# Expert rows moved by index tables, and rope halves exchanged by on-chip DMA, in a two-layer mixer and MoE trunk

## The reference

```python
h = layer_norm(x)
for l in range(2):
    m = hybrid_mixer(h, ...)           # three attentions d, s, f, gated, w_o
    h = layer_norm(ALPHA * h + m)
    f = grouped_moe(h, ...)
    h = layer_norm(ALPHA * h + f)
```

## Time and profile before

| what | value |
|---|---|
| runs | 2792.02 us median of 3 (2791.88 to 2793.4) |
| profiled execution | 2794.2 us, its span 2792.3 us |
| PE busy | 2209.5 us (79%) |
| DVE, ACT, POOL busy | 920.5, 532.5, 206.2 us |
| DMA moved | 569.59 MB, mean 204 GB/s |
| mean granted PE clock | 0.906 of full speed |

### The profile page before, as it was taken

How to read it: one execution, slowest core, us unless ns; L and a number is a source line. 1 busy time by engine, 2 the same in 40 slices (tenths; PEclk the granted TensorE clock), 3 DMA queues, 4 the chain that set the end, 5 groups by cost and what they waited for, 6 DMA issues and landing times.

```text
span 2792.3 us, 29623 instructions
## 1 busy us (share of the span) xinstructions
PE 2209.5 (79%) x9808; PEld 1253.0 (45%) x9816; DVE 920.5 (33%) x1844; ACT 532.5 (19%) x1132; POOL 206.2 (7%) x354
## 2 busy tenths in 40 slices
PE   4889979989938777777478899799898477777772
PEld 3656746756413222222156567467564122222221
DVE  5656542452331010010255564424524201000004
ACT  2342242242010000000032412412410100000000
POOL 1000010000011000000200000100000100001003
PEclk9999978999969998999779999799999699899995
DMA  9401200301159999999722022013022699999992
GB/s 341 157 31 58 94 31 31 121 31 56 50 210 393 401 395 394 400 402 401 256 105 91 1 91 91 1 62 119 16 91 93 246 404 399 403 403 396 402 396 97
DMA packets 95754, 569.59 MB, mean 204 GB/s; under 512 B 13472, under 2 KB 16288, under 8 KB 71072
## 3 DMA queue, kind: packets, MB, share of 16 engines
q1 hardware_dynamic: 73696, 494.31, 45.5%
q0 software_dynamic: 21952, 73.94, 7.3%
HBM read 524.70 MB, written 43.52 MB: 203 GB/s over the span
## 4 chain that ended last, share of the span: by engine, by line
PE 56%; DMA 23%; DVE 8%; issue 6%; ACT 4%; POOL 1%; SPq 1%; ACTq 0%; DVEq 0%; POOLq 0%
DMA xslot<-in_w_up 19%; PE ps L839 11%; PE ps L584 9%; PE ps L585 8%; PE ps L586 8%; PE ps L778 6%; PE ps L792 4%; PE ps L855 2%; DVE small L1302 2%; ACT scr L1031 2%; PE ps L745 2%; DMA ring<-in_w_gate 2%; PE ps L706 1%; PE ps L615 1%; PE ps L728 1%
## 5 line engine op out<-in xcount | busy, mean ns | idle before, releaser
L839 PE MATMUL ps<-ring,scr 128*64 128x512 f32 x1024 | 499.8, 645 | 150.6 <-issue 67.6
L584 PE MATMUL ps<-hT_lo,w_hi 128*128 128x512 f32 (+1 forms) x832 | 359.2, 432 | 28.3 <-DVE w_lo L1176 24.5
L839 PEld LDWEIGHTS ps<-ring,scr 128*64 128x64 f32 x1024 | 146.9, 148 | 484.7 <-issue 412.2
L1592 DVE TENSOR_TENSOR scr<-scr,ps 64x512 f32<-64x512 f32 x64 | 44.3, 691 | 953.2 <-ACT scr L1126 953.2
L585 PE MATMUL ps<-hT_hi,w_lo 128*128 128x512 f32 (+1 forms) x832 | 329.1, 396 | 0.0
L586 PE MATMUL ps<-hT_hi,w_hi 128*128 128x512 f32 (+1 forms) x832 | 328.8, 395 | 0.0
L961 ACT ACTIVATE scr<-ps 128x512 f32<-128x512 f32 (+3 forms) x334 | 148.8, 460 | 731.4 <-PE ps L855 392.2
L840 PE MATMUL ps<-ring,scr 128*64 128x512 f32 x512 | 260.2, 667 | 0.0
L840 PE MATMUL ps<-xslot,scr 128*64 128x512 f32 x512 | 239.9, 624 | 0.0
L1176 DVE TENSOR_TENSOR w_lo<-ring,w_hi 128x1024 fp32r<-128x1024 f32 (+1 forms) x128 | 155.4, 1218 | 184.8 <-ACT w_hi L981 175.4
L584 PEld LDWEIGHTS ps<-hT_lo,w_hi 128*128 128x128 f32 (+1 forms) x832 | 158.9, 191 | 82.0 <-DVE w_lo L1176 26.2
(11 more groups left out here) (203 smaller groups left out, 2576.4 us busy)
## 6 DMA issues: line engine op xcount, KB each, us to landing
ring<-in_w_gate SPq DMA_DIRECT2D x64, 2048.0 KB, 19.2
ring<-in_w_up SPq DMA_DIRECT2D x32, 2048.0 KB, 23.6
ring<-in_w_down SPq DMA_DIRECT2D x32, 2048.0 KB, 23.2
xslot<-in_w_up SPq DMA_DIRECT2D x32, 2048.0 KB, 25.7
xslot<-in_w_down SPq DMA_DIRECT2D x32, 2048.0 KB, 26.2
ring<-in_w_in SPq DMA_DIRECT2D x30, 2048.0 KB, 8.3
scr<-x_rows POOLq DMA_DIRECT2D x68, 256.0 KB, 9.2
y_rows<-scr POOLq DMA_DIRECT2D x128, 128.0 KB, 7.5
```

The source lines that it names most:

```text
L584: mm(out, a[0], b[1], start=first, stop=False)
L839: mm(bank[b].t[0:C, :], xT[n][:, k, :], wg[:, k, :], start=(k == 0), stop=(k == KD - 1))
```

## The change

1. The exchange of rope halves leaves PE. Behind each z copy ACT waits for the copy and issues four DMAs from SBUF to SBUF, each of 32 partitions by 512 floats (64 KB), into z_turned (double-buffered). DVE's second product reads z_turned after a wait for the four landings. `turn_halves` and the permutation constant are gone.
2. x_rows is gone. POOL writes h to h_rows (2 MB in HBM) with four direct DMAs after ln1. Routing no longer ends with slots; DVE builds for each (token, choice) a one-hot row of its place in a block (row_hot) and a row with 2 * (choice * 512 + token) + 1 in the column of its block (blk_val), and PE multiplies them, 8 pairs for each of two halves of the output. The result, 128 by 47, holds what lies in each place of each block, and 0 for an empty one. `indices` on DVE turns it into two tables: the row of h to fetch, and the half row of y_halves to write; empty places get an index beyond the bound. The schedule of overflow blocks is computed behind that.
3. In the expert loop POOL copies one column of a table and issues an indirect DMA: a gather of up to 64 rows (4 KB each) from h_rows, a scatter of up to 128 half rows (2 KB each) to y_halves. Indices out of bounds are skipped.
4. y_halves is ordered by choice and token, so that combine is fed by four direct DMAs of 1 MB. The zero fill is gone, with DVE's wait for it. ACT's scaling of h waits for the four writes of h instead of the scatters.

```diff
@@ PE, projections (turn_halves and roped_blocks removed)
+                def projected(keys, l, name):
+                    for n, key in enumerate(keys):
+                        project(key, l, name, n)
@@ PE, route
+                    pe.wait_ge(dve_seq.sem, dve_seq.at("places", l))
+                    free(5, l)
+                    for k in range(2):
+                        for t in range(NT):
+                            for half in range(2):
+                                ins = mm(bank[5].t[half * C:(half + 1) * C, 0:NBLK], row_hot[:, k, t, :],
+                                         blk_val[:, k, t, :], start=(k + t == 0), stop=(k == 1 and t == NT - 1))
+                    filled(ins, 5, "places")
@@ ACT, take_z
                     copy(z[r % 2], b, bank[b].t, scale)
+                    in_sbuf(b, key, l)
+                    alone(act)
+                    for p0 in range(0, P, 32):
+                        act.dma_start(z_turned[r % 2][p0:p0 + 32, :], z[r % 2][p0 ^ 32:(p0 ^ 32) + 32, :]).then_inc(
+                            turn_land[r % 2].sem, turn_land[r % 2].tick(r, 16))
@@ ACT
-                    act.wait_ge(scattered.sem, scattered.at("all", l))
+                    act.wait_ge(rows_written.sem, rows_written.at("all", l))
-                                act.wait_ge(y_stored[n].sem, y_stored[n].start(l, i) + 32)
+                                act.wait_ge(y_stored[n].sem, y_stored[n].start(l, i) + 16)
@@ DVE, rope
-                    b = 4 + r % 2
-                    filled(b, ("rope", r), l)
-                    V.tensor_tensor(r2, bank[b].t, sin, ALU.mult).then_inc(bank[b].read, 1)
-                    dve.wait_ge(dve_seq.sem, dve_seq.now(l))
-                    in_sbuf(b, ("rope", r), l)
+                    dve.wait_ge(turn_land[r % 2].sem, turn_land[r % 2].at(r, l))
+                    link(V.tensor_tensor(r2, z_turned[r % 2], sin, ALU.mult), l)
@@ DVE, route
-                    L(V.scalar_tensor_tensor(slotf, r8a, float(C), slotf, ALU.mult, ALU.add))
-                    V.tensor_copy(slot_keep[:, :, :], slotf).then_inc(slot_ready.sem, slot_ready.tick("slot"))
+                    N(V.tensor_tensor(row_hot.rearrange("p k t c -> p (k t) c"),
+                                      iota_c.unsqueeze(1).to_broadcast([P, 2 * NT, C]),
+                                      slotf.rearrange("p k t -> p (k t)").unsqueeze(2).to_broadcast([P, 2 * NT, C]),
+                                      ALU.is_equal))
+                    for k in range(2):
+                        for t in range(NT):
+                            N(V.tensor_scalar(blk_val[:, k, t, :], iota_c[:, 0:NBLK], r8a[:, k, t:t + 1],
+                                              place[:, k, t:t + 1], ALU.is_equal, ALU.mult))
@@ DVE, new
+                def indices(l):
+                    filled(5, "places", l)
+                    at = bank[5].t[:, 0:NBLK]
+                    V.tensor_scalar(empty, at, 0.0, 1e6, ALU.is_equal, ALU.mult).then_inc(dve_seq.sem, dve_seq.tick())
...
+                    V.tensor_copy(y_idx, y_at).then_inc(index_ready.sem, index_ready.tick("y"))
+                    dve.wait_ge(dve_seq.sem, dve_seq.now(l))
+                    V.tensor_copy(x_idx, x_at[0:C, :]).then_inc(index_ready.sem, index_ready.tick("x"))
@@ POOL
+                def column(now, idx, blk, l=0, i=NTURN - 1):
+                    G.tensor_copy(now, idx[:, blk]).then_inc(pool_seq.sem, pool_seq.tick())
+                    pool.wait_ge(pool_seq.sem, pool_seq.now(l, i))
+                    alone(pool)
+                def gather_rows(n, sig, key=None):
+                    pool.indirect_dma_start(
+                        out=xin[n], out_offset=None, in_=h_rows,
+                        in_offset=bass.IndirectOffsetOnAxis(ap=x_now[n], axis=0),
+                        bounds_check=T - 1, oob_is_err=False).then_inc(sig.sem, sig.tick(key, 16))
+                def scatter_rows(n, sig, key=None):
+                    pool.indirect_dma_start(
+                        out=y_halves, out_offset=bass.IndirectOffsetOnAxis(ap=y_now[n], axis=0),
+                        in_=ysb[n], in_offset=None,
+                        bounds_check=4 * T - 1, oob_is_err=False).then_inc(sig.sem, sig.tick(key, 16))
...
-                    for k in range(2):
-                        for t in range(NT):
-                            pool.indirect_dma_start(
-                                out=x_rows, out_offset=bass.IndirectOffsetOnAxis(ap=slot_keep[:, k, t:t + 1], axis=0),
-                                in_=h[:, t, :], in_offset=None).then_inc(scattered.sem, scattered.tick("all", 16))
-                    pool.wait_ge(scattered.sem, scattered.at("all", l))
-                    alone(pool)
-                    load_rows(l, 0, slice(0, C))
-                    load_rows(l, 1, slice(C, 2 * C))
+                    for n in range(2):
+                        column(x_now[n], x_idx, slice(n, n + 1), l)
+                        gather_rows(n, xin_land[n], "x")
...
-                            load_rows(l, e % 2, bass.ds((i * EPT + e + 2) * C, C), i)
+                            column(x_now[e % 2], x_idx, bass.ds(i * EPT + e + 2, 1), l, i)
+                            gather_rows(e % 2, xin_land[e % 2], "x")
...
-                            store_rows(n, bass.ds((i * EPT + e) * C, C), y_stored[n], "y")
+                            column(y_now[n], y_idx, bass.ds(i * EPT + e, 1), l, i)
+                            scatter_rows(n, y_stored[n], "y")
...
+                    y_of = y_halves.rearrange("(k t p h) c -> t p k (h c)", k=2, p=P, h=2)
                     for t in range(NT):
-                        for k in range(2):
-                            pool.indirect_dma_start(
-                                out=got[t][k], out_offset=None, in_=y_rows,
-                                in_offset=bass.IndirectOffsetOnAxis(ap=slot_keep[:, k, t:t + 1], axis=0)).then_inc(
-                                got_land[t].sem, got_land[t].tick(t, 16))
+                        pool.dma_start(scr[:, 6144 + t * 2048:8192 + t * 2048].rearrange("p (k d) -> p k d", k=2),
+                                       y_of[t]).then_inc(got_land[t].sem, got_land[t].tick(t, 16))
```

More of the change, by code:

```diff
@@ L168, in trunk @@
         ring = sb("ring", [P, RING, PIECE])
-        cf = sb("cf", [P, 2 * P + NEXP * 2 + 3])
+        cf = sb("cf", [P, P + C + NEXP + 4 + 2 * NT])
         cb = sb("cb", [P, 5 * P + 8], BF16)
[L171 to L174, removed]
+        ident = cf[:, 0:P]
+        iota_e = cf[:, P:P + NEXP]
+        iota_c = cf[:, P:P + C]
+        iota_g = cf[:, P + C:P + C + NEXP]
+        c0 = P + C + NEXP
+        half_less = cf[:, c0 + 3:c0 + 4]
+        place = cf[:, c0 + 4:c0 + 4 + 2 * NT].rearrange("p (k t) -> p k t", k=2)
         inv_freq, sign_half, m_half = cf[:, c0:c0 + 1], cf[:, c0 + 1:c0 + 2], cf[:, c0 + 2:c0 + 3]
@@ L252, in trunk @@
         wts, rank, quo, bas, slotf, r8a, r8b, wsum = k8
-        slot = scr[:, RT + 1360:RT + 1368].bitcast(U32).rearrange("p (k t) -> p k t", k=2)
+        row_hot = scr[:, 6144:6144 + 2 * NT * C].rearrange("p (k t c) -> p k t c", k=2, c=C)
+        blk_val = scr[:, 6656:6656 + 2 * NT * NBLK].rearrange("p (k t b) -> p k t b", k=2, b=NBLK)
+        empty, second, y_at, x_at = (scr[:, 7168 + NBLK * n:7168 + NBLK * (n + 1)] for n in range(4))
+        x_idx = scr[0:C, 16384:16384 + NBLK].bitcast(U32)
+        y_idx = scr[:, 16448:16448 + NBLK].bitcast(U32)
+        x_now = [scr[0:C, 16512 + n:16513 + n].bitcast(U32) for n in range(2)]
+        y_now = [scr[:, 16514 + n:16515 + n].bitcast(U32) for n in range(2)]
         ovt = scr[0:1, RT + 1368:RT + 1368 + NOV * NEXP].rearrange("p (j e) -> p j e", e=NEXP)
@@ L295, in trunk @@
         roped = signal("roped")
+        turn_land = [signal(f"turn_land{n}") for n in range(2)]
         ffe_ready = signal("ffe_ready")
@@ L319, in trunk @@
         over_w = signal("over_w")
+        over_col = signal("over_col")
         over_x = signal("over_x")
@@ L551, in _ @@
                 mm = nc.tensor.matmul
-                turn = {"pj": 0, "rope": 0}
-                rope_src = {}
+                turn = {"pj": 0}
                 def free(b, l=0, i=0):
@@ L1576, in _ @@
                     route(l)
+                    indices(l)
+                    schedule(l)
                     def rows(e, i=0):
@@ L1784, in constants @@
     i = np.arange(P)
-    swap = np.zeros((P, P), np.float32)
-    swap[i ^ 32, i] = 1.0
     tri = (i[:, None] < i[None, :]).astype(np.float32)
     e = np.tile(np.arange(NEXP, dtype=np.float32), (P, 1))
+    c = np.tile(np.arange(CAP, dtype=np.float32), (P, 1))
+    place = 2.0 * (np.arange(2 * NT)[None, :] * P + i[:, None]) + 1.0
     freq = np.float32(10000.0) ** (-np.arange(0, HD, 2, dtype=np.float32) / np.float32(HD))
@@ L1794, in constants @@
         pick[32 * part + np.arange(8), np.arange(8)] = -1.0
-    cf = np.concatenate([np.eye(P, dtype=np.float32), swap, e,
```

(3 more changed lines are left out.)

86 lines of the change are left out of this document (34 added, 52 removed).

## The result

| kernel | median us | range | ratio to before | 95% interval |
|---|---|---|---|---|
| before | 2791.95 | 2791.25 to 2793.4 (4 runs) | | |
| after | 2696.09 | 2693.57 to 2702.82 (4 runs) | 0.9661 | 0.9645 to 0.9676 |

A forecast was written before the change was run, and what follows sets the result against it. PE was taken to bound the mixers, DMA the expert loop, with serial stretches between. Gains of 31 (rope), 13 (routing) and 24 (loop) sum to 68 us, giving 2724 us; own range 2705 to 2740, wider range 2700 to 2762.

The forecast's parts named there:

- term 3: Expert loop: only filled places move, half the row traffic; 12 us per layer, 24 in two.
- balance: Expert loop: the slowest of 16 engines completes a weight piece; one may keep all its rows, so the middle was taken.
- rival (c): Expert loop gets all of the halving, 21 us per layer: 2706 us; chance 0.10.
- Rope halves: Mixers: swap matmuls leave PE for DMAs issued by ACT; 15.5 us per layer, 31 in two.
- the term of the four issues: Mixer, ACT: four transfers issued after each z copy at 0.5 us each, ending at S+2.65, S being the copy's start.
- The estimate of 2.2 us in the prediction: Mixer: one 64 KB transfer by the skill page, never late, no stall; rope gain 33 instead of 31 us.
- the prediction's signs of being wrong: PE waiting for w_lo in d and s; DVE over 1 us for turned halves; loop at 17.0; ACT waiting for stores.
- Rival (b): Rope groups: ACT becomes the late engine with issues of 1.0 us; gain 5 instead of 31, 2750 us; chance 0.13.
- Routing to first rows: Between mixer and loop: new series of 12.5 us, 7 saved; 6.5 taken per layer, 13 in two.
- Loop end to combine: After the loop: last store 0.9 us later, fetch back 0.9 earlier; net 0 (-3 to +3).
- Zero fill: Mixers: removing the fill wins nothing, as windows with and without it last 733 and 732 us.
- Rival (d): Mixers: turned halves land late behind weights; slower than before from landings of 11.1 us in every block; chance 0.06.

The follow-up runs named there:

- spread: The kernel after with each expert's rows dealt to places in steps of four, so filled places don't stand together: 2698.26 us, 0.9665.
- no_skip: The kernel after with empty places not skipped: they fetch some row of h and store to spare rows behind y_halves; 2757.77 us, 0.9880.
- pe_swap: The kernel after with the rope halves exchanged by PE again, as before the change: 2704.15 us, 0.9681.
- hi_first: The kernel after with ACT's next w_hi split put between the z copy and the four DMA issues: 2682.88 us, 0.9613.
- no_loads: The kernel after with no row loaded in the expert loop (all gathers skip all), stores as in after: 2633.21 us, 0.9433.
- skip_stores: The kernel after with empty places skipped only in the stores; all loads move, empty ones fetching some row of h: 2751.08 us, 0.9857.
- no_rows: The kernel after with every place declared empty: no row loaded or stored in the expert loop, y_halves filled once at the start; 2611.57 us, 0.9353.

## Why the prediction was off

The direction and the large parts were right, the size of the loop was not. The step that failed is term 3: it priced a row at the time that its own packets take in q0 (0.72 us per expert for half of loads and stores), and then halved that again for balance, to 12 per layer. Measured are 30.3 and 28.0 per layer, because a load also makes the weights' packets longer, a path that the term didn't have. That the total missed by only 28 us is partly luck: by the table of stretches the loop was priced 34 too low and the stretches between 14 too low, the mixer 16 too high.

- **Loop.** Both halves of the step fell. Balance costs nothing (spread), so rival (c), the whole of the halving, is nearest with 21 per layer. It too is short, because loads and stores aren't equal: with the other already halved, half of the loads is worth 26.5 us per layer (521.2 - 494.7; q0's own 30 us in two layers and as much again in weight packets that got shorter), half of the stores 6.1 (500.8 - 494.7; q0's own 17 in two layers). Taken first, from no_skip, they are worth 22.4 and 2.0; either order makes the whole 28.5 (22.4 + 6.1, 2.0 + 26.5). Bounds made of q0's own time alone could not hold this.
- **Rope halves.** Mechanism right, price off: the term of the four issues was mis-sized. The forecast said where it would turn: at an issue of 0.6 "the chain is 0.1 us late in every second block". It took 0.61, and w_lo ended at S+5.6 where S+5.0 was counted: the first issue begins at S+0.7 (0.65 counted), the four take 2.45 (2.0 counted), and 0.1 passes before the split. The projections came 0.65 and 0.83 late. Besides, landings were not 3 us where it mattered. From the chain of after:

```profile
64.81 4.55 DMA scr<-scr
...
331.52 7.17 DMA scr<-scr
...
548.01 6.68 DMA scr<-scr
```

The median is 2.5 us. Of the 152 in the packed trace of after, the 72 beside which the weights' queue held under 0.05 of the 16 engines' time landed in 2.05 us in the median (3.4 at most); the 40 that took over 4 us all ran while it held at least 0.59, and these are waited for. The estimate of 2.2 us in the prediction, from the Trainium skill's "DMA: Bandwidth & Descriptors", section Anatomy of one DMA, agrees with the quiet ones alone; the fit of that section is of DMAs issued by GpSimd, not by ACT. d and s kept 13.2 of 27.8 us in two layers. The index blocks, counted at a gain of 3.2 in two layers, lost 4.7 (26.4 and 26.9 before, 29.2 and 28.8 after, from the first projection to the logits): with one projection between the last z copy (62.27) and the logits (70.93) the chain of issue, landing and rope took 8.7 where 7.4 were counted, and the first group of four issues took 3.39 us; the stretch from the first logits to the next projection gave 2.6 back. pe_swap has the whole term at 8 to 10 us. Two of the prediction's signs of being wrong were there: PE waited for w_lo inside d and s, and DVE for turned halves, 3.5 us at the longest. Rival (b) had named the late engine; it was half true.
- **Routing to first rows.** Forecast 12.5 from the slot arithmetic, measured 10.3; gain 9.2 instead of 7 in this piece, 18.2 in two layers instead of 13. The 32 matmul pieces took 1.95 (3.5 counted, from pieces of 128 columns), the gather 3.15 from issue to use (4.8 counted, from a scatter), the small compares 1.79 (1.3).
- **Loop end to combine.** Counted at nothing; 1.1 and 5.7 came. The stretch from the last down projection to the first sum is 1.8 shorter in layer 0, half of which the prediction had counted for the fetch and then given away again for the store. In layer 1 it is 2.1 shorter (18.7 and 16.6), and the rest of the 5.7 lies at the very end: from the issue of the last output to the end of the span pass 14.3 us before and 10.7 after. Why was not taken apart.
- **Zero fill.** Forecast nothing. No run separates it; pe_swap's mixers (731.1 and 730.7) leave 2 us each against before for everything in the mixer but the swaps, and layer 1, which had no fill, has as much as layer 0. That agrees.
- **Rival (d),** late landings that cost more than all gains: landings did reach 7.2 us and hi_first shows DVE held at them for 5.6, but its deciding point of 11.1 in every block was never near.

What stays open is why a row load stretches the weights' packets and a row store doesn't. The loads are read from HBM and written to SBUF, as the weights are; the stores go the other way. The packets' size is hardly it: a half row has 2 KB, but of the 1020 store packets with data in layer 0's loop of no_loads the packed trace has 992 at 4 KB, the size of a load packet. So the direction is the likelier cause, which is argued and not shown: no run here turns it alone. The direct loads of before (loop 523.8 in the mean) cost as much as the indirect ones (523.2), so the indirect form isn't it.

## What to carry over

In a loop that the DMA engines bound, price a small transfer beside a stream by what the stream loses too, not by the time of its own packets: here half of the row loads cost the loop 1.7 to 2.9 times their own packets' time, half of the stores 0.2 to 1.1 times theirs. A DMA issued by a computing engine is that engine's work (0.6 us each on ACT), so put what another engine waits for ahead of it; and where its landing has a long tail, move the reader back one step rather than count on the median. When one late engine is cured, look for the wait it had covered: the split first brought 13 us, the later read another 7.

## What the runs showed of the hardware

- Row loads in DMA-bound loops made 494 MB of weight packets take 1284, 1254 and 1219 us of 16 engines' time at all, half and none of the loads (skip_stores, after, no_loads). No run shows that fewer stores shorten them.
- Places with an index beyond the bound move nothing: q0 carried 53.49 MB with all places and 35.69 with the filled ones, and the loop shortened with it, while POOL's issue stayed at about 1.0 us. A skipped place leaves a packet record of some 9 ns (no_rows: q0 2.8 us in a loop).
- An issue from ACT took 0.61 us, against 0.36 busy at a pitch of 0.55 on SP; a group of four took 2.45, in 4 of the 38 groups of after 3.1 to 3.5.
- An ACT copy of 32 partitions by 512 from PSUM to other partitions of SBUF took 0.59 us, four in a row 2.43, about the same as one of 128 partitions (0.60).
- SBUF to SBUF transfers of 64 KB landed in 2.05 us in the median with next to no weight traffic, in up to 7.2 beside it.
